# Paged decode attention: cache pages by indirect transfers, transposed on VectorE, scored in 32x32 tiles

## The chip, the cores and the metric

One core of one Trainium2 chip runs the whole program, one launch. The metric is the device time of that launch in microseconds (us), lower is better. A core has TensorE (PE, with its weight loads as PEld), VectorE (DVE), ScalarE (ACT), GpSimd (POOL) and SyncE (SP), which run their own instruction streams and meet at semaphores. All matrices are float32.

## What is computed

One inference step of a two-layer hybrid decoder: a diagonal state-space layer, then an attention layer that reads one shared compressed latent cache. It runs for a prompt of 512 tokens and for eight decode sequences of one new token each, whose 2048 past positions lie in pages. Cut to the part at issue, per decode sequence:

```
c_past   = cache_ckv[page_table]   # (8, 2048, 256), pages of 128 positions
kpe_past = cache_kpe[page_table]   # (8, 2048, 32)
s   = (q_lat @ c^T + q_pe @ kpe^T) * 96**-0.5      # 16 heads x 2049 keys
o   = softmax(s) @ c                                # 16 x 256
out = (o per head @ w_uv) @ w_o
```

Around it stand four SwiGLU feed-forward blocks, the state-space mixer, projections and norms, in three-product split precision.

## The kernel before, in words

Everything is written by hand per engine, in program order, with explicit semaphores. Prompt and decode tokens share the big products (520 columns). After the latent queries are ready, PE runs the prompt attention over eight pairs of heads (`scores`, `turned_probs`, `weighted`), and then the decode attention over eight sequences, called batches (b = 0..7) here. The output projection `w_o` follows; its first halves (`wo_half(d, 0, ...)`, 24 matmuls each, line 3209) are placed between the last steps of decode.

**Loads.** `page_loader` (before line 654) reads page numbers into registers and loads a batch's 16 pages of 128x256 into `cb[b % 3]` and 16 key pages of 128x32 into `kb[b % 3]`, split over SP (9 pages) and POOL (7), key loads at line 639. Partition p holds position p of each page. Three buffers: the load of b+3 waits until the weighted sum of b is done (`d_o`); that of batch 2 waits for the end of the prompt attention (`a_ol`).

**Decode, per batch.** PE transposes the pages with an identity (`turned`, line 2401: 36 of 128x128 in nine groups, the last for the keys) into PSUM banks 0, 1, 7; ACT (lines 1489, 1491) and DVE (line 2247) copy them in turn to `cbT` and `kbT`. Scores: line 3223 (8 matmuls of 32x512, in four column tiles, one for each quarter of the keys) and line 3227 (16 of 32x128). DVE takes the maximum (2291, 2292), ACT the exponential with the row sum (1532), PE turns the probabilities (4 transposes), DVE copies them (2301), and PE forms the weighted sum (line 3258, 16 matmuls of 32x256), which ACT copies out (1537). The PE order in round b is scores of b, first transposes of b+1, probabilities of b, other transposes of b+1, weighted sum of b:

```python
            for b in range(NB):
...
                if b + 1 < NB:
                    for q in range(4):
                        turned(b + 1, q)
...
                pe.wait_ge(d_e, b + 1)
...
                if b + 1 < NB:
                    for q in range(4, 9):
                        turned(b + 1, q)
```

A float32 matmul shows as two records in the trace.

## Time and profile before

| | us |
|---|---|
| median of 3 runs | 2009.85 |
| lowest and highest run | 2007.43, 2014.37 |
| span of the profiled execution | 2007.1 |
| PE / DVE / ACT / POOL busy | 1960.4 / 1277.0 / 820.4 / 132.8 |

The span runs from the first to the last instruction of the profiled execution; its own run time is not given apart from it, and the span is 0.33 us under the lowest run. Busy times are sums of an engine's work; a line number such as L3258 is that of the kernel above, and where a helper issues the instruction it is the helper's. Idle time of an engine that nobody waits for costs nothing.

### The profile page before, as it was taken

The numbers are of one execution on the slowest core, as the hardware profiler recorded it, in microseconds if no ns is written. First come the engines' busy times: TensorE is split into PE (matmuls) and PEld (weight loads), VectorE is DVE, ScalarE is ACT, GpSimd is POOL, SyncE is SP. The second block draws the span as 40 slices with busy tenths as digits, with TensorE's granted clock in tenths as the row PEclk, the third lists the DMA queues.
The fourth block names the chain that finished last, engine by engine and source line by source line (L and its number), as shares of the span: only waits on it lengthen the run. The fifth ranks groups of instructions, "written<-read, shape, count | busy, mean of one in ns | idle before, by whom it ended". The sixth has DMA issues, their size and how long they took to land.

```text
span 2007.1 us, 41612 instructions
## 1 busy us (share of the span) xinstructions
PE 1960.4 (98%) x17604; PEld 1875.2 (93%) x17604; DVE 1277.0 (64%) x1771; ACT 820.4 (41%) x1243; POOL 132.8 (7%) x231
## 2 busy tenths in 40 slices
PE   8999999988999999999999999999989999999999
PEld 7999999987999999999999999997666799999998
DVE  6445486697469577576884856655764349668474
ACT  5332233343245244255452534454654244345252
POOL 3002002010000000000000000000047000000000
PEclk9999999989999999999999999999999999999999
DMA  7233234864342322234322322231248422323222
GB/s 151 84 102 88 75 93 115 269 140 100 95 137 85 120 89 95 77 105 116 97 85 85 127 85 86 84 101 51 54 119 231 149 71 83 127 85 120 91 74 75
DMA packets 260624, 211.55 MB, mean 105 GB/s; under 512 B 42372, under 2 KB 235426, under 8 KB 260450
## 3 DMA queue, kind: packets, MB, share of 16 engines
q1 hardware_dynamic: 248528, 187.52, 31.9%
q0 software_dynamic: 6656, 13.69, 2.4%
q10 hardware_dynamic: 5266, 7.85, 1.2%
q8 instruction: 130, 2.13, 0.4%
q14 instruction: 44, 0.36, 0.1%
HBM read 195.29 MB, written 10.33 MB: 102 GB/s over the span
## 4 chain that ended last, share of the span: by engine, by line
PE 67%; DVE 3%; ACT 2%; issue 2%; SPq 1%; DMA 1%; DVEq 0%; ACTq 0%
PE ps L2459 25%; PE ps L2487 25%; PE ps L2388 6%; PE ps L2401 2%; PE ps L2947 1%; PE ps L3053 1%; PE ps L3209 1%; PE ps L3086 1%; SPq L654 1%; SPq L639 1%; DMA cb<-cache_ckv 1%; PE ps L2841 1%; PE ps L3030 1%; DVE wl L1668 0%; DVE xl L1619 0%
## 5 line engine op out<-in xcount | busy, mean ns | idle before, releaser
L2388 PE MATMUL ps<-xh,wh 128*128 128x260 f32 x1088 | 286.9, 285 | 2.6 <-DVE xl L1619 1.4
L2388 PE MATMUL ps<-xl,wh 128*128 128x260 f32 x1088 | 283.7, 283 | 0.0
L2487 PE MATMUL ps<-xoh,wh 128*128 128x260 f32 x992 | 281.3, 284 | 1.3 <-DVE sq L1835 1.3
L2487 PE MATMUL ps<-xoh,wl 128*128 128x260 f32 x992 | 281.0, 283 | 0.0
L2487 PE MATMUL ps<-xol,wh 128*128 128x260 f32 x992 | 280.6, 283 | 0.0
L2459 PE MATMUL ps<-xh,wh 128*128 128x260 f32 x872 | 228.8, 284 | 0.6 <-DVE wl L1668 0.6
L1067 ACT ACTIVATE wh<-rw 128x1024 fp32r<-128x1024 f32 (+1 forms) x135 | 138.8, 1029 | 218.6 <-PE ps L2459 151.7
L2459 PE MATMUL ps<-xl,wh 128*128 128x260 f32 x872 | 227.0, 282 | 0.0
L2388 PE MATMUL ps<-xh,wl 128*128 128x260 f32 x1088 | 219.3, 283 | 0.0
L990 ACT ACTIVATE wh<-raw 128x1024 fp32r<-128x1024 f32 (+1 forms) x90 | 100.4, 1116 | 283.4 <-PE ps L2388 250.5
L2388 PEld LDWEIGHTS ps<-xh,wh 128*128 128x128 f32 x1088 | 205.6, 189 | 6.9 <-issue 3.9
L2388 PEld LDWEIGHTS ps<-xl,wh 128*128 128x128 f32 x1088 | 205.1, 188 | 0.0
L1668 DVE TENSOR_TENSOR wl<-rw,wh 128x1024 fp32r<-128x1024 f32 (+1 forms) x135 | 160.3, 1188 | 67.3 <-ACT wh L1067 67.2
L2487 PE MATMUL ps<-xoh,third 128*128 128x260 f32 x1040 | 198.6, 283 | 0.6 <-DVE sq L1835 0.6
L2487 PEld LDWEIGHTS ps<-xoh,wh 128*128 128x128 f32 x992 | 186.6, 188 | 1.6 <-DVE wl L1668 1.6
L2487 PEld LDWEIGHTS ps<-xol,wh 128*128 128x128 f32 x992 | 186.9, 188 | 0.0
L2487 PEld LDWEIGHTS ps<-xoh,wl 128*128 128x128 f32 x992 | 186.8, 188 | 0.0
L1579 DVE TENSOR_TENSOR wl<-raw,wh 128x1024 fp32r<-128x1024 f32 (+1 forms) x92 | 120.5, 1310 | 89.5 <-ACT wh L990 81.8
L2459 PE MATMUL ps<-xh,wl 128*128 128x260 f32 x872 | 175.5, 283 | 0.0
L2388 PEld LDWEIGHTS ps<-xh,wl 128*128 128x128 f32 x1088 | 167.9, 189 | 0.0
L2459 PEld LDWEIGHTS ps<-xh,wh 128*128 128x128 f32 x872 | 164.4, 189 | 1.7 <-DVE wl L1668 1.1
L2487 PEld LDWEIGHTS ps<-xoh,third 128*128 128x128 f32 x1040 | 164.8, 188 | 0.8 <-DVE third L1668 0.8
(550 smaller groups left out, 4202.2 us busy)
## 6 DMA issues: line engine op xcount, KB each, us to landing
rw<-ffn_w_gate SPq DMA_DIRECT2D x33, 1024.0 KB, 5.4
rw<-ffn_w_up SPq DMA_DIRECT2D x33, 1024.0 KB, 8.0
rw<-ffn_w_down SPq DMA_DIRECT2D x12, 2048.0 KB, 7.8
raw<-ffn_w_gate SPq DMA_DIRECT2D x22, 512.0 KB, 3.9
raw<-ffn_w_up SPq DMA_DIRECT2D x22, 512.0 KB, 3.9
raw<-ffn_w_down SPq DMA_DIRECT2D x16, 704.0 KB, 4.8
rw<-ffn_w_down SPq DMA_DIRECT2D x6, 1536.0 KB, 6.7
cb<-cache_ckv SPq DMA_DIRECT2D x72, 128.0 KB, 3.7
```

The source lines that it names most:

```text
L639: eng.dma_start(kb[j][:, g, :], inp["cache_kpe"][bass.ds(numbers[b][g], 1)].rearrange("a p r -> p (a r)")).then_inc(arrived[j], 16)
L654: eng.dma_start(cb[j][:, g, :], inp["cache_ckv"][bass.ds(numbers[b][g], 1)].rearrange("a p r -> p (a r)")).then_inc(arrived[j], 16)
L990: run(wh[par_][:, 0:size], raw[par_][:, 0:size], ACT.Copy).then_inc(w_hi, 1)
L1067: run(as_slot(name, slot_h(name, n), n), raw_of(name, n), ACT.Copy).then_inc(z_hi, 1)
L1579: tt(wl[par_][:, 0:size], raw[par_][:, 0:size], wh[par_][:, 0:size], ALU.subtract).then_inc(w_lo, 1)
L1668: tt(as_slot(name, slot_l(name, n), n), raw_of(name, n), as_slot(name, slot_h(name, n), n), ALU.subtract).then_inc(z_lo, 1)
L2388: got = mm(ps[0:width, bank + half, 0:HALF], w[par_][:, k * width:k * width + width], src[:, k0 + k, half * HALF:half * HALF + HALF], star ...
L2401: return nc.tensor.transpose(dst, src, ident[0:rows, 0:rows])
L2459: got = mm(ps[:, bank + half, T0], w[:, cols], src_[:, k, half * HALF:half * HALF + HALF], start=first and m == 0 and s == 0, stop=last an ...
L2487: got = mm(ps[:, bank + mat, T0], w[:, cols], src[:, j, k, :], start=first and k == 0 and m == 0 and s == 0, stop=k == 3 and m == 1, skip_ ...
L2841: got = mm(ps[:, bank + half, 0:HALF], w[slot][:, k * P:k * P + P], src[:, k, half * HALF:half * HALF + HALF], start=k == 0 and m == 0 and ...
L2947: got = mm(ps[:, 2 * (i % 2) + half, 0:HALF], cols, src[:, k, half * HALF:half * HALF + HALF], start=k == 0 and o == 0 and s == 0, stop=k ...
```

## The change

The caches are viewed as rows of 16 positions, so that one indirect transfer per batch and cache, on POOL, brings page rows straight to the partitions: partition p holds positions 16p to 16p+15. The row numbers (page number times 8 plus p % 8) are made once, from the page table, which POOL loads in eight small transfers at the start. DVE transposes `cb` and `kb` in 32x32 blocks from SBUF to SBUF, five operations a batch (`turned(b, k)`, four of 128x1024, one of 128x512). The scores are 9 x 16 matmuls of 32 rows, 32 columns and 128 keys (`cache_scores`): row group i works on the positions that partitions 32i to 32i+31 held, 32 of the 256 + 32 dimensions at a time, and writes PSUM bank i; column group c takes four of the 16 positions of each partition. For this the queries stand four times, once per row group, in `qrep`: SP copies them from `qlat` with 16 transfers (`latent_rows`), in place of its register loads. The new token's scores have 16 columns per batch rather than 32. ACT, not DVE, copies the turned probabilities. The weighted sum of b now stands after the scores of b+1, and the projection's halves and banks are placed anew.

```diff
-SP_PG = 9
-N_SP, N_POOL = 2 * SP_PG - 1, 2 * (NPG - SP_PG) + 1
-AHEAD = 5
-LAST_EARLY = 5
+SLOT = PAST // P
+SUBS = PAGE // SLOT
 SCALE = float(DQ) ** -0.5
 HP = 32
 NQ = P // HP
 KB = PAST // NQ
+NJ = R // DR + 1
+PAIRS = tuple((2 * k, 2 * k + 1) for k in range(R // DR // 2)) + ((NJ - 1,),)
+NT = len(PAIRS)
+WO_BANK = ((7, 4), (1, 0), (2, 5), (3, 6))
 NEG = -1e30
...
-            qlat, qpe, snew = take(s, ("qlat", [P, RT, NB, HP], F32), ("qpe", [P, NB, 4, HP], F32),
-                                   ("snew", [NB, NB, HP], F32))
+            qlat, qrep, snew = take(s, ("qlat", [P, RT, NB, NH], F32), ("qrep", [P, NJ, NB * NH + NH], F32),
+                                    ("snew", [NB, NB, HP], F32))
...
-                    m, ("cbT", [P, RT, PAST], F32), ("cb2", [P, NPG, R], F32), ("mb", [P, NB], F32), ("nmb", [P, NB], F32),
+                    m, ("cbT", [P, NJ - 1, KB], F32), ("cb2", [P, NPG, R], F32), ("mb", [P, NB], F32), ("nmb", [P, NB], F32),
...
-        kbT = tb[:, 0, 0:4 * P].rearrange("p (g k) -> p g k", g=4)
+        kbT = tb[:, 0, 0:KB]
...
-        def page_loader(eng, arrived, ckv, kpe):
...
-                for g in kpe:
-                    eng.dma_start(kb[j][:, g, :], inp["cache_kpe"][bass.ds(numbers[b][g], 1)].rearrange("a p r -> p (a r)")).then_inc(arrived[j], 16)
...
-                for g in ckv:
-                    eng.dma_start(cb[j][:, g, :], inp["cache_ckv"][bass.ds(numbers[b][g], 1)].rearrange("a p r -> p (a r)")).then_inc(arrived[j], 16)
...
+            def latent_rows(i):
+
+                if i == 0:
+                    sp.wait_ge(l_qe, 1)
+                for q in range(NQ):
+                    sp.dma_start(qrep[DR * i:DR * i + DR, q:NJ - 1:NQ, 0:NB * NH],
+                                 qlat[DR * q:DR * q + DR, :, :, :].rearrange("p r b h -> p r (b h)")).then_inc(d_q, 16)
+
...
-                if i - 2 < AHEAD:
-                    number(i - 2)
+                if i - 2 < NQ:
+                    latent_rows(i - 2)
             load(WO0 + 1, (WO0 + 1) % 2, wo[:, :, P:2 * P], KD)
 
-            caches()
             sp.wait_ge(d_o, NB - 2)
...
+            def cache_out(b):
+                act.wait_ge(d_o, b + 1)
+                run(ob[:, b, :], ps[:, 5 + b % 2, 0:R], ACT.Copy).then_inc(d_oe, 1)
 
             for b in range(NB):
-                if b + 1 < NB:
-                    turned(b + 1, 0)
-                else:
-                    act.wait_ge(d_o, NB - 1)
-                    for j in range(2):
-                        act.wait_ge(w_in[(WO0 + j) % 2], slots.arrived(WO0 + 2 + j))
-                        run(w4h[:, j, :], raw[(WO0 + j) % 2][:, 0:KD * P], ACT.Copy).then_inc(w_hi, 1)
-
                 act.wait_ge(d_m, b + 1)
                 if b >= 1:
                     act.wait_ge(d_pt2, b)
-                run(pb, ps[:, 2 + b % 2, :], ACT.Exp, bias=nmb[:, b:b + 1], scale=SCALE, accum_out=lb[:, b:b + 1]).then_inc(d_e, 1)
-                if b + 1 < NB:
-                    for q in range(2, 9, 2):
-                        turned(b + 1, q)
-                act.wait_ge(d_o, b + 1)
-                run(ob[:, b, :], ps[:, 5 + b % 2, 0:R], ACT.Copy).then_inc(d_oe, 1)
+                run(pb.rearrange("p (m i k) -> p i m k", m=NQ, i=NQ),
+                    ps[:, 0:NQ, 0:P].rearrange("p i (m k) -> p i m k", m=NQ),
+                    ACT.Exp, bias=nmb[:, b:b + 1], scale=SCALE, accum_out=lb[:, b:b + 1]).then_inc(d_e, 1)
+                if b >= 1:
+                    cache_out(b - 1)
+                act.wait_ge(d_pt2, b + 1)
+                run(pbT[:, :, :], ps[:, 4, :].rearrange("p (m q) -> p m q", m=NQ), ACT.Copy).then_inc(d_pe, 1)
             act.wait_ge(d_w, 1)
             run(mrow[:, :, :], mrow[:, :, :], ACT.Exp, scale=SCALE)
             run(nrow[:, :], nrow[:, :], ACT.Exp, scale=SCALE).then_inc(d_we, 1)
+            for j in range(2):
+                act.wait_ge(w_in[(WO0 + j) % 2], slots.arrived(WO0 + 2 + j))
+                run(w4h[:, j, :], raw[(WO0 + j) % 2][:, 0:KD * P], ACT.Copy).then_inc(w_hi, 1)
+                if j == 0:
+                    cache_out(NB - 1)
...
-                    last = copy(qpe[DR * k:DR * k + DR, :, k, Q_POS[h]:NH:4], qq[DR * h:DR * h + DR, NH // 2:NQT, SEQ:TOK].rearrange("p g b -> p b g"))
+                    last = copy(qrep[DR * k:DR * k + DR, NJ - 1, 0:NB * NH].rearrange("p (b h) -> p b h", b=NB)[:, :, Q_POS[h]:NH:4], qq[DR * h:DR * h + DR, NH // 2:NQT, SEQ:TOK].rearrange("p g b -> p b g"))
...
+            def turned(b, k):
+
+                if k == 0:
+                    dve.wait_ge(d_in[b % 3], (b // 3 + 1) * 16)
+                elif k == NT - 1:
+                    dve.wait_ge(d_kin[b % 3], (b // 3 + 1) * 16)
                 if b >= 1:
-                    dve.wait_ge(d_s, b)
-                copy(cbT[:, q // 4, (q % 4) * 512:(q % 4) * 512 + 512], ps[:, (0, 1, 7)[(b * 9 + q) % 3], :]).then_inc(d_td, 1)
+                    dve.wait_ge(d_s, (b - 1) * NT + k + 1)
+                if k == NT - 1:
+                    V.transpose(kbT, kb[b % 3][:, :, :].rearrange("p s e -> p (s e)")).then_inc(d_t, 1)
+                else:
+                    j0, j1 = PAIRS[k][0], PAIRS[k][-1] + 1
+                    V.transpose(cbT[:, j0:j1, :].rearrange("p j (s k) -> p j s k", k=DR),
+                                cb[b % 3][:, :, DR * j0:DR * j1].rearrange("p s (j e) -> p j s e", e=DR)).then_inc(d_t, 1)
 
             for i in range(NH // 2):
                 more = i + 1 < NH // 2
...
-            turned(0, 3)
-            turned(0, 5)
+            turned(0, 1)
             weighted(NH // 2 - 1)
-            turned(0, 7)
+            for k in range(2, NT):
+                turned(0, k)
...
-                dve.wait_ge(d_s, b + 1)
-                own(V.tensor_reduce(mb[:, b:b + 1], ps[:, 2 + b % 2, :], AX.X, ALU.max))
+                if b + 1 < NB:
+                    turned(b + 1, 0)
+                dve.wait_ge(d_s, (b + 1) * NT)
+                own(V.tensor_reduce(mb[:, b:b + 1], ps[:, 0:NQ, 0:P], AX.XY, ALU.max))
                 ts(nmb[:, b:b + 1], mb[:, b:b + 1], -SCALE, None, ALU.mult).then_inc(d_m, 1)
                 if b + 1 < NB:
-                    turned(b + 1, 1)
-                    turned(b + 1, 3)
-                else:
-                    wide_lo(0)
-                dve.wait_ge(d_pt2, b + 1)
-                if b >= 1:
-                    dve.wait_ge(d_o, b)
-                copy(pbT[:, :, :], ps[:, 4, :].rearrange("p (m q) -> p m q", m=NQ)).then_inc(d_pe, 1)
-                if b + 1 < NB:
-                    turned(b + 1, 5)
-                    turned(b + 1, 7)
+                    for k in range(1, NT):
+                        turned(b + 1, k)
                 if b == 1:
                     dve.wait_ge(l_rdy, 1)
                     eye = ident[0:NB, 0:NB].unsqueeze(2).to_broadcast([NB, NB, HP])
...
+            def cache_scores(b, k):
+
+                if b == 0 and k == 0:
+                    pe.wait_ge(d_q, 16 * NQ * NQ)
+                    pe.wait_ge(a_e, NH // 2 * NSS)
+                pe.wait_ge(d_t, b * NT + k + 1)
+                for j in PAIRS[k]:
+                    for c in range(NQ):
+                        for i in range(NQ):
+                            rows = slice(DR * i, DR * i + DR)
+                            keys_ = kbT if j == NJ - 1 else cbT[:, j, :]
+                            got = mm(ps[HP * c:HP * c + HP, i, 0:P], qrep[rows, j, NH * b:NH * b + HP], keys_[rows, P * c:P * c + P],
+                                     start=j == 0, stop=j == NJ - 1, skip_group_check=True)
+                got.then_inc(d_s, 1)
...
-            for q in range(2, 6):
-                turned(0, q)
+            cache_scores(0, 0)
             weighted(NH // 2 - 1)
-            for q in range(6, 9):
-                turned(0, q)
+            for k in range(1, NT):
+                cache_scores(0, k)
...
+            def cache_weighted(b):
...
+            for b in range(NB):
+                if b >= 1:
+                    cache_weighted(b - 1)
+                pe.wait_ge(d_e, b + 1)
+                for m in range(NQ):
+                    got = turn(ps[:, 4, m * P:m * P + P], pb[:, m * P:m * P + P])
+                got.then_inc(d_pt2, 1)
+                if b + 1 < NB:
+                    for k in range(NT):
+                        cache_scores(b + 1, k)
+            turn(ps[0:NB, 0, 0:P], mb[:, :])
+            turn(ps[0:NB, 0, P:2 * P], lb[:, :]).then_inc(d_rt, 1)
+            pe.wait_ge(a_ol, NH // 2)
+            wo_half(0, 0, 0, 3)
+            cache_weighted(NB - 1)
+            wo_half(0, 0, 3, KD)
             pe.wait_ge(d_ws, 1)
             turn(ps[:, 4, 0:NB], mrow[:, :, :].rearrange("p q h -> p (q h)"), NB)
-            mm(ps[:, 7, NB * HP:2 * NB * HP], ones[0:NB, :], own_w[:, :, :].rearrange("p b h -> p (b h)"), start=True, stop=True).then_inc(d_wp, 1)
-            wo_half(2, 0, 3, 5)
+            mm(ps[:, 0, NB * HP:2 * NB * HP], ones[0:NB, :], own_w[:, :, :].rearrange("p b h -> p (b h)"), start=True, stop=True).then_inc(d_wp, 1)
+            wo_half(1, 0, 0, 3)
...
+            for c in range(SUBS):
+                pool.dma_start(pt[c:P:SUBS, :], inp["page_table"].rearrange("b g -> g b"), allow_slow_non_contiguous=True).then_inc(d_pt, 16)
...
+            G.memset(qrep[:, :, NB * NH:NB * NH + NH], 0.0)
+            G.memset(snew[:, :, :], 0.0).then_inc(m_zero, 1)
+            pool.wait_ge(d_pt, 16 * SUBS)
+            pool.wait_ge(c_in, 48)
+            own(G.tensor_scalar(slot_row[:, :], pt[:, :], float(SUBS), cst[:, C_SUB:C_SUB + 1], ALU.mult, ALU.add))
+
+            def rows_of(b):
+                return bass.IndirectOffsetOnAxis(ap=slot_row[:, b:b + 1], axis=0)
+
+            def keys(b):
+
+                j = b % 3
+                if b >= 3:
+                    pool.wait_ge(d_t, NT * (b - 2))
+                pool.indirect_dma_start(kb[j][:, :, :].rearrange("p s e -> p (s e)"), None,
+                                        inp["cache_kpe"].rearrange("n (u s) e -> (n u) (s e)", s=SLOT), rows_of(b)).then_inc(d_kin[j], 16)
+
+            def pages(b):
+
+                j = b % 3
+                if b == 0:
+                    pool.wait_ge(a_qs[0], 64 * (NH // 4))
+                    pool.wait_ge(a_qs[1], 64 * (NH // 4))
+                elif b == 1:
+                    pool.wait_ge(a_ve, NH // 2)
+                elif b == 2:
+                    pool.wait_ge(a_ol, NH // 2)
+                else:
+                    pool.wait_ge(d_o, b - 2)
+                pool.indirect_dma_start(cb[j][:, :, :].rearrange("p s r -> p (s r)"), None,
+                                        inp["cache_ckv"].rearrange("n (u s) r -> (n u) (s r)", s=SLOT), rows_of(b)).then_inc(d_in[j], 16)
+
+            for b in range(NB):
+                pages(b)
+                if b < 2:
+                    keys(b)
+                if b == 1:
+                    keys(2)
+                if 2 <= b < NB - 1:
+                    keys(b + 1)
```

Where instructions move, as the built programs list them (line, operation, output and inputs, shape, awaited semaphores, count). PE before, from the last transposes of batch 1 over the weighted sum of batch 0 to the scores of batch 1 (`cb`, `kb` are cache pages, `ta` the probabilities, `cst` the identity):

```order
L2401 MATMUL ps<-cst,cb 128x128 [waits dec_tr_d]
L2401 MATMUL ps<-cst,cb 128x128 x3
L2401 MATMUL ps<-cst,cb 128x128 [waits dec_tr_a]
L2401 MATMUL ps<-cst,cb 128x128 x3
L2401 MATMUL ps<-cst,kb 128x128 [waits dec_tr_d]
L2401 MATMUL ps<-cst,kb 128x128 x3
L3258 MATMUL ps<-cb,ta 32x256 [waits dec_p_sb]
L3258 MATMUL ps<-cb,ta 32x256 x15
L3223 MATMUL ps<-cbT,qlat 32x512 [waits dec_tr_d,dec_tr_a]
L3223 MATMUL ps<-cbT,qlat 32x512 x7
```

PE now, from the last scores of batch 1 over the weighted sum of batch 0 to the first scores of batch 2:

```order
L3106 MATMUL ps<-cbT,qrep 32x128 [waits dec_tr]
L3106 MATMUL ps<-cbT,qrep 32x128 x31
L3106 MATMUL ps<-tb,qrep 32x128 [waits dec_tr]
L3106 MATMUL ps<-tb,qrep 32x128 x15
L3160 MATMUL ps<-cb,ta 32x256 [waits dec_p_sb]
L3160 MATMUL ps<-cb,ta 32x256 x15
L2345 MATMUL ps<-cst,ta 128x128 [waits dec_exp]
L2345 MATMUL ps<-cst,ta 128x128 x3
L3106 MATMUL ps<-cbT,qrep 32x128 [waits dec_tr]
```

The transposes of `cb` are gone, and the weighted sum (`cb,ta`) stands behind the scores of the next batch (`cbT,qrep`) and ahead of the turned probabilities of that batch.

DVE before, one round (`mb` is the maximum, `ta` the turned probabilities):

```order
L2291 TENSOR_REDUCE mb<-ps 128x1 [waits dec_s]
L2292 TENSOR_SCALAR nmb<-mb 128x1 [waits dch]
L2247 COPY cbT<-ps 128x512 [waits dec_s,dec_tr] x2
L2301 COPY ta<-ps 128x512 [waits dec_o,dec_p_tr]
L2247 COPY cbT<-ps 128x512 [waits dec_s,dec_tr] x2
```

DVE now:

```order
L2196 STREAM_TRANSPOSE cbT<-cb 128x1024 [waits dec_s,dec_in1]
L2243 TENSOR_REDUCE mb<-ps 128x1 [waits dec_s]
L2244 TENSOR_SCALAR nmb<-mb 128x1 [waits dch]
L2196 STREAM_TRANSPOSE cbT<-cb 128x1024 [waits dec_s] x3
L2193 STREAM_TRANSPOSE tb<-kb 128x512 [waits dec_s,pool_in1]
```

A block transpose of the next batch, which waits for that batch's load (`dec_in1`), stands ahead of the maximum; four more follow it.

POOL now (it had 7 page and 8 key loads a batch here):

```order
L3409 DMA cb<-cache_ckv,slot_row 128x4096 [waits att_ol]
L3394 DMA kb<-cache_kpe,slot_row 128x512 [waits dec_tr]
L3409 DMA cb<-cache_ckv,slot_row 128x4096 [waits dec_o]
L3394 DMA kb<-cache_kpe,slot_row 128x512 [waits dec_tr]
L3409 DMA cb<-cache_ckv,slot_row 128x4096 [waits dec_o]
```

Each page load waits for a weighted sum (`dec_o`), and the key load one batch ahead follows it.

## Rows read from the trace of the kernel before

**Rows 1.** The page: span, and section 1 (busy, share, instructions).

```profile
span 2007.1 us, 41612 instructions
...
PE 1960.4 (98%) x17604; PEld 1875.2 (93%) x17604; DVE 1277.0 (64%) x1771; ACT 820.4 (41%) x1243; POOL 132.8 (7%) x231
```

**Rows 2.** Windows: busy us (instructions) of PE, PEld, DVE, ACT, POOL; clock, DMA share, GB/s.

```profile
1515.00:1525.00 10.00, 9.99 (x128) 7.05 (x131) 4.91 (x9) 4.15 (x10) 7.65 (x15) 1.00 0.61 166
1525.00:1535.00 10.00, 9.49 (x128) 6.70 (x124) 5.23 (x10) 4.00 (x9) 9.19 (x18) 1.00 1.00 274
```

**Rows 3.** Waits, 1500 to 1600: us in total, times, longest.

```profile
DVE mb L2291 <- PE ps L3227: 32.4, 8, 4.3
...
PE ps L2401 <- DMA cb<-cache_ckv: 2.1, 3, 1.0
```

**Rows 4.** Chain of waits, 1490 to 1640: start, us, what.

```profile
1534.78 1.86 PE ps L3258 x32
1536.64 1.72 PE ps L3223 x16
1538.36 0.87 PE ps L3227 x32
1539.23 1.93 PE ps L2401 x16
1541.18 2.98 PE ps L2401 x24
...
1573.95 1.86 PE ps L3258 x32
...
1577.53 0.88 PE ps L3227 x32
```

**Rows 5.** Timeline, 1495 to 1535: start, us, engine, line, what.

```profile
1506.30 0.69 DVE L2235 TENSOR_TENSOR xl<-ps,xh 128x512 fp32r<-128x512 f32 x1 [2.25 <-ACT xh L1478]
...
1515.41 1.93 PE L3258 MATMUL ps<-cb,ta 128*32 128x256 f32 x32
```

**Rows 6.** Groups by form, 1495 to 1620: count, busy us, mean ns, idle before.

```profile
L2401 PE MATMUL ps<-cst,cb 128*128 128x128 f32 x256 | 31.8, 276 | 2.1 <-DMA cb<-cache_ckv 2.1
...
L654 POOL DMA_DIRECT2D cb<-cache_ckv x42 | 22.6, 537 | 22.6 <-issue 20.1 <-PE ps L3258 0.8
...
L2291 DVE TENSOR_REDUCE mb<-ps 128x1 f32<-128x512 f32 x8 | 5.5, 691 | 32.4 <-PE ps L3227 32.4
...
L1532 ACT ACTIVATE ta<-ps,nmb 128x512 f32<-128x512 f32 x8 | 5.5, 682 | 1.2 <-DVE nmb L2292 1.2
...
L2287 DVE TENSOR_TENSOR w4l<-raw,w4h 128x1024 fp32r<-128x1024 f32 x2 | 2.4, 1220 | 0.0
...
L2292 DVE TENSOR_SCALAR nmb<-mb 128x1 f32<-128x1 f32 x8 | 1.2, 154 | 0.3
```

**Rows 7.** Small tiles: line 2853 (ns min/median/max), and a group by form.

```profile
L2853 PE MATMUL ps<-sn,ct x128: 201/201/221, 443.7 to 445.4; 128*32 128x8 f32 x128
...
L2817 PE MATMUL ps<-ctcw,xsr 64*64 64x128 f32 x256 | 7.9, 272 | 4.9 <-DVE xsr L740 4.8
```

**Rows 8.** DMA issues: count, KB each, median us to landing.

```profile
rw<-ffn_w_down SPq DMA_DIRECT2D x12, 2048.0 KB, 7.8
...
wsh<-s_w_rows POOLq DMA_DIRECT2D x1, 4096.0 KB, 23.3
```

**Rows 9.** Windows of 2 us, columns as in rows 2.

```profile
1492.00:1494.00 2.00, 0.22 (x2) 0.20 (x4) 1.90 (x9) 1.37 (x5) 1.71 (x4) 1.00 0.38 62
1496.00:1498.00 2.00, 2.00 (x12) 1.31 (x9) 0.08 (x1) 0.60 (x1) 0.00 (x0) 0.50 0.00 0
1598.00:1600.00 2.00, 2.00 (x11) 2.00 (x11) 0.46 (x3) 0.26 (x1) 0.00 (x0) 0.50 0.06 18
```

**Rows 10.** Chain of waits, the output projection.

```profile
1585.10 3.09 PE ps L3209 x24
...
1597.75 5.80 PE ps L3209 x36
```

More of the change, by code:

```diff
@@ L87 @@
 C_E4 = C_S32 + HP
-C_COLS = C_E4 + NQ
+C_SUB = C_E4 + NQ
+C_COLS = C_SUB + 1
 C_GRP, C_ALL = C_COLS, C_COLS + D
@@ L287, in yoco_step @@
         wl = take(ctx, *[(f"wl{j}", [P, HF * P], F32R) for j in range(2)])
[L290 removed]
+        be0, lst, pt, slot_row = take(ctx, ("be0", [P, KD, P], F32), ("lst", [P, 3, 4, NPAIR], F32), ("pt", [P, NB], I32), ("slot_row", [P, NB], I32))
         with ExitStack() as s:
@@ L1452, in _ @@
             act.wait_ge(l_s, 1)
-            run(snew[:, :, :], ps[0:NB, 6, 0:NB * HP].rearrange("p (b h) -> p b h", b=NB), ACT.Copy).then_inc(l_rdy, 1)
+            act.wait_ge(m_zero, 1)
+            run(snew[:, :, 0:NH], ps[0:NB, 6, 0:NB * NH].rearrange("p (b h) -> p b h", b=NB), ACT.Copy).then_inc(l_rdy, 1)
             def softmax(i, n):
@@ L1481, in _ @@
                 softmax(0, n)
-            def turned(b, q):
-                act.wait_ge(d_t, b * 9 + q + 1)
-                if b >= 1:
-                    act.wait_ge(d_s, b)
-                src = ps[:, (0, 1, 7)[(b * 9 + q) % 3], :]
-                if q < 8:
-                    run(cbT[:, q // 4, (q % 4) * 512:(q % 4) * 512 + 512], src, ACT.Copy).then_inc(d_ta, 1)
-                else:
-                    run(kbT[:, :, :], src.rearrange("p (g k) -> p g k", g=4), ACT.Copy).then_inc(d_ta, 1)
             for i in range(NH // 2):
@@ L2252, in _ @@
                     maximum(i + 1, 0)
+                else:
+                    turned(0, 0)
                 if i == 0:
@@ L2268, in _ @@
                     normalise(i + 1, 2)
-                else:
-                    turned(0, 1)
                 probs(i, 5)
@@ L2328, in _ @@
                ps[:, 4, 0:NB].unsqueeze(2).to_broadcast([P, NB, HP]), ALU.mult).then_inc(d_fin, 1)
-            own(copy(nwt[:, :, :], ps[:, 7, NB * HP:2 * NB * HP].rearrange("p (b h) -> p b h", b=NB)))
+            own(copy(nwt[:, :, :], ps[:, 0, NB * HP:2 * NB * HP].rearrange("p (b h) -> p b h", b=NB)))
             wide_lo(1)
@@ L3185, in _ @@
                 turned_probs(i, 3)
-                if not more:
-                    turned(0, 0)
                 turned_probs(i, 4)
-                if not more:
-                    turned(0, 1)
                 turned_probs(i, 5)
```

143 lines of the change are left out of this document (19 added, 124 removed).

## The prediction

> **What bounds the kernel now.** The page comes first [rows 1]: TensorE (PE) is busy for 98% of the span of 2007.1 us, so work that is taken from it counts, unless a wait takes its place. The change touches one stage, the decode attention of eight sequences ("batches" here), so the windows of that stage come next [rows 2]: the granted clock is 1.00 (2.4 GHz), PE is busy 9.5 to 10 of 10 us, and the DMA share is 0.61 to 1.00 at 166 to 274 GB/s. Two limits therefore lie close together, and relief of one meets the other. The waits say the same [rows 3]: VectorE (DVE) stands 32.4 us waiting for PE's scores, while PE waits 2.1 us for cache pages, three times.
>
> The chain of waits gives one batch in steps [rows 4]: weighted sum 1.86 us, scores against the latent 1.72, scores against the rotary key 0.87, 1.93 for 16 transposes and 2.98 for 24 more (20 of the cache, 4 of the probabilities). The weighted sum of batch 0 begins at 1515.41 [rows 5] and that of batch 6 at 1573.95 [rows 4]: 58.54 us over 6 is **9.76 us a batch**. The scores of batch 7 end at 1577.53 + 0.88 = **1578.4**, the mark of my sum. After it the output projection keeps PE supplied, as it will afterwards.
>
> **The change, part by part.**
>
> *Transposes leave PE.* 36 of 128x128 a batch at 31.8 us / 256 for the latent [rows 6], 0.124, hence 4.5 us of PE. Their nine evacuations on ACT and DVE go too.
>
> *Scores in small tiles.* 24 matmuls (2.6 us in rows 4) become 9 x 16 = 144 of 32x32 tiles and 128 columns; each shows as two records, 288 a batch. The rotary scores, four column tiles of 128 columns at once, took 0.87 us for 32 records [rows 4], 0.109 for four. If sixteen run at once, 18 groups take **2.0 us**; if only four do, 72 groups take 7.8. The nearest rows [rows 7]: 64x64 tiles, two row groups and two column groups at once, 256 records in 7.9 us busy, which without row concurrency would need twice that; and 128 small records within 1.7 us, 13 ns each. 288 x 13.3 ns is 3.8 us. I take 2.0 to 3.8: either is hidden beside the next part, and 7.8 is a rival.
>
> The same row speaks to a rule against this change. The Trainium skill (TensorE: Matmul & The Clock Gate, section "Wait — 56ns, not 53.3ns?") says that where instructions are not decoded in hardware the sequencer spends about 62 ns on each matmul. By that rule 144 matmuls would be an estimated 8.9 us a batch and the kernel would be slower. The 13 ns a record of rows 7, 27 a matmul, speak against it here.
>
> *Transposes on DVE.* Four of 128x1024 and one of 128x512 a batch. No such operation is in the trace. The nearest are a DVE operation from SBUF on 128x1024, 1220 ns, and the maximum, 691 ns for 512 out of PSUM [rows 6]. I take 1.15 us and 0.6; the bounds are 0.6 us (twice that rate) and 2.2 us (half of it). With the maximum (0.69 + 0.15) DVE has 4 x 1.15 + 0.6 + 0.85 = 6.0 us a batch, under 9.76.
>
> *Order.* DVE now has the first transpose of batch b+1 ahead of the maximum of batch b, so that softmax b waits for the landing L of b+1. From L: 1.15 + 0.85 + 3 x 1.15 + 0.6, and 0.3 for the last matmuls: scores b+1 end at L + 6.35. Only then comes the weighted sum of b, w = 1.86 at full clock, which releases the buffer that load b+3 waits for. The old order had that sum ahead of the next scores. With T from issue to landing, **L(b+3) = L(b+1) + 6.35 + w + T**: two batches per round.
>
> *The loads.* 16 page loads and 16 key loads a batch from two queues become two indirect ones from POOL. SP and POOL issues (0.54 us each on POOL [rows 6]) vanish; but nothing starts before the buffer is free, and the whole 2 MB must land before the first transpose. The nearest rows [rows 8]: 2048 KB from SP lands in 7.8 us; a 4096 KB load from POOL's queue in 23.3, that is 11.7 for half. I take **T = 8.4**, nearest to the first, which has the same size, with 7.0 (the 2.36 MB at somewhat over the 274 GB/s of rows 2, and no more) and 11.7 as ends. The data alone, 2.36 MB at the 274 GB/s of rows 2, would be 8.6 a batch, as much as the loop above (6.35 + 2.35 + 8.4 over two batches, 8.55), so a second limit stands close behind; larger pieces should pass it. The skill (DMA: Bandwidth & Descriptors, section "Anatomy of one DMA — SWDGE (gpsimd) path") gives 2.0 us plus bytes over 436 GB/s, an estimated 6.8 us for this load; by it the sum would be about 5 us lower. No row here reaches that rate.
>
> *PE's clock.* From the weighted sum's end, L(b) + 8.7, to the turned probabilities, L(b+1) + 2.8, PE will idle 2 to 3 us a batch. In the trace a gap of this kind left its mark [rows 9]: PE busy 0.22 of 2 us at 1492, and a granted clock of 0.50 (1.2 GHz) at 1496, with PE fully busy. At that level a weighted sum takes 3.7; I take w = 2.35, a quarter of them low. The projection will also start low once: where the clock fell to 0.50 at 1598 [rows 9], 36 records took 5.80 us against 3.09 for 24 at 1585 [rows 10], that is 1.2 us more than their share.
>
> *Head.* The DVE evacuation of the last prompt head begins at 1506.30 [rows 5]; without cache transposes ahead of the last weighted sum it should be 1.3 us sooner, ending at 1505.7. Three transposes follow (1.15, 1.15, 0.6), so that scores 0 end at 1508.8. The first transpose of 1 (to 1509.7), the maximum (to 1510.6) and the rest give scores 1 at 1515.0, weighted sum 0 at 1516.8 and the issue of load 3 there. L(3) = 1516.8 + T. Load 2 (from 1505.7 to 1514.1) is in time. The new token's scores shrink from 256 to 128 columns: 3 x 0.2, 0.6 us saved. The page-table issues on POOL, the replication of queries by SP (16 small DMAs) and the removed register loads lie in those queues' idle time: nothing.
>
> *Sum.* L(7) = L(3) + 2 x (6.35 + w + T); after it scores 7 (6.35) and weighted sum 6 (w), which stood before the mark in the old order: 1516.8 + 19.05 + 3 x (w + T) = 1535.9 + 3 x 10.75 = 1568.1, against 1578.4: -10.3. With -0.6 and +1.2: **-9.7 us**, a span of 1997.4. The span of 2007.1 is 2.75 below the median of 2009.85 (the lowest run is 2007.43), so the median becomes **2000.2**. The last few tens of microseconds hold no other change: softmax 7 hides behind weighted sum 6, and the chain from row sums to weights (about 4.3 us) behind half a projection tile (3.09 for 24 records, [rows 10]) and a weighted sum, 4.9.
>
> **Rivals.**
>
> 1. *Loads slow.* The indirect load needs 11.7 us or more, as the POOL row suggests. Each microsecond of T costs three: 3 x 3.3 = 9.9, hence +0.2 us, 2010.1, no change; at 14 us it would be +7.1, 2017. For: it is the same queue. Against: the SP row, and that the 4096 KB load is cut into short rows. Chance 0.16.
>
> 2. *Slower: DVE becomes the bound.* A transposed block of 4-byte elements passes at half the rate, 2.2 us per 1024. Then DVE has 4 x 2.2 + 1.1 + 0.85 = 10.8 us a batch. Scores 0 end at 1512.5, scores 7 at 1512.5 + 7 x 10.8 = 1588.1, with w 1589.9: +11.5, with -0.6 and +1.2 **+12.1, 2022.0**. It decides from about 1.6 us per transpose on. For: no row shows the operation. Against: every DVE row here runs near one element per cycle and lane. Chance 0.13.
>
> 3. *Small tiles bind PE.* They run four at a time, or their issue is the limit: 7.8 us of scores, with 0.44 and 1.86 10.1 a batch on PE. Scores 0 would end near 1511: 1511 + 7 x 10.1 + 1.9 = 1583.6, 5.2 past the mark, less 0.6: +4.6, 2014.5. Rows 7 speak against it. Chance 0.07. The 62 ns of the page above would be this rival, somewhat dearer.
>
> 4. *Everything fast.* T at 7.0 and w at 1.86, as PE stays at 2.4 GHz: 1535.9 + 26.6 = 1562.5, -15.9, with -0.6 and no low start -16.5, 1993.3. For: the 1 KB pieces of before cost more per byte than long ones should. Chance 0.12. The 6.8 us of the page above lead here.
>
> **How the numbers follow.** My forecast has 0.52. About 6 us (0.3%) is what a measurement of this kernel can tell from no change; the forecast's own spread of T (up to 10) gives 2005.0 at its upper end, so some of it counts as no change. Faster: 0.45 of the forecast and all of rival 4, 0.57. No change: 0.07 of the forecast, 0.10 of rival 1, 0.02 of rival 3, 0.19. Slower: the rest of these, 0.11, and rival 2, 0.24. The range runs from 1993 (rival 4) to 2018 (rival 1 at 14 us) and leaves out most of rival 2.
>
> **What would show it.** Right: STREAM_TRANSPOSE groups of 1.1 to 1.2 us; score records at 7 to 14 ns; cache loads landing in 8 to 9 us; 8.5 us from one weighted sum to the next; PE idle 2 to 3 us a batch, ended by DVE's transposes after a DMA; a granted clock under 1 in the stage. Wrong: landings of 11 us and more, transposes of over 1.6 us, or DVE never waiting for a load; also a clock that stays low far into the projection, which I count at 1.2 us only.

## The result, and the profile after

The changed kernel takes a median of 2033.4 us (2030.06 to 2037.92, 4 runs) against 2009.34 us (2007.43 to 2014.37, 4 runs) before it: ratio 1.0114, 95% interval 1.0096 to 1.0131. It is slower by 24 us, where 2000.2 was forecast, and lies above the range. The profiled run took 2030.06 us, its span is 2028.2.

The page, sections 1 and 2, against [rows 1]:

```profile
span 2028.2 us, 43625 instructions
...
PE 1954.6 (96%) x19236; PEld 1868.7 (92%) x19236; DVE 1290.5 (64%) x1771; ACT 802.4 (40%) x1211; POOL 87.7 (4%) x136
```

TensorE has 1632 matmul records more and is busy 6 us less, in a span that is 21 us longer: it stands still. The windows say where, columns as in [rows 2]:

```profile
1515.00:1525.00 10.00, 9.08 (x309) 5.40 (x294) 6.29 (x9) 1.76 (x4) 1.91 (x2) 0.63 0.12 25
1525.00:1535.00 10.00, 4.75 (x200) 2.93 (x180) 2.59 (x4) 0.58 (x1) 0.00 (x0) 0.71 0.53 218
```

PE was busy 9.99 and 9.49 us here, now 9.08 and 4.75, and its clock is low for over half of the time. What it waits for, 1500 to 1600 (us in total, times, longest), against [rows 3]:

```profile
ACT ta L1468 <- DVE nmb L2244: 73.8, 8, 10.7
POOL cb L3409 <- PE ps L3160: 55.7, 5, 14.4
DVE cbT L2196 <- DMA cb<-cache_ckv,slot_row: 34.4, 6, 7.7
...
PE ps L3106 <- issue: 23.3, 8, 5.2
```

L3106 is the score matmul of 32x32, L3160 the weighted sum, L2196 the transpose on DVE. The last row is the finding: for 23.3 us PE waited at a score matmul for nothing that another engine owed it ("issue"); a ninth wait of that kind, 2.4 us, lies inside a weighted sum, so **25.7 us** in all. The waits of DVE, ACT and POOL follow from it only in part: in fewer_scores below, which has no such gap, they are still 19.8, 54.6 and 39.0 us, from the order and the loads. The chain of waits over one batch, against [rows 4]:

```profile
1522.47 0.59 PE ps L2345 x4
1523.06 3.83 PE ps L3106 x208
1526.88 5.25 issue
1532.13 0.74 PE ps L3106 x31
1532.87 3.48 PE ps L3160 x32
```

For scores and weighted sum a batch needs 3.83 + 0.74 + 3.48, and 5.25 us of nothing between two score matmuls of the rotary keys, the first of which had already run. The weighted sum of batch 0 begins at 1518.90, that of batch 6 at 1595.23 and ends at 1598.24:

```profile
1518.90 3.57 PE ps L3160 x32
...
1595.23 3.01 PE ps L3160 x32
1598.24 0.80 PE ps L2345 x6
```

That is (1595.23 - 1518.90) / 6 = **12.7 us a batch** instead of 9.76, and the mark is 1598.24 instead of 1578.4, 19.8 later. From the mark to the end of the span it is 430.0 us against 428.7 before. Of the 21.1 us by which the span grew, 19.8 lie ahead of the mark.

The DMA view of 1500 to 1600 offers a cause: a queue of its own carries instructions, in packets of 16384 bytes. After, then before (packets, MB, share):

```profile
q8 instruction: 20, 0.33, 1.3%
```

```profile
q8 instruction: 10, 0.16, 0.7%
```

TensorE's program holds 648 instructions a batch now (576 of scores: each matmul has two weight loads and two passes; 64 of the weighted sum, 8 of turns) and 240 before. 240 in 9.76 us with a packet every 10 us makes about 250 instructions a packet (an estimate), so that a batch now needs 2.6 packets. In the trace two packets never begin less than 3.3 us apart. Where a cache load begins, the next packet starts 5.9 to 8.4 us after the one before, and the one after it 3.5 to 4.8 us later. Eight of the nine gaps end 1.3 to 1.5 us after a packet is in, the ninth 1.0. For the gap of 5.25 us, 1526.88 to 1532.13: from 1521.5 to 1529.5 the DMA view lists the load and no packet of q8, and from 1529.5 to 1532.2 it lists the one after which PE goes on:

```profile
q0 software_dynamic: 119, 1.95, 64.5%
```

```profile
q0 software_dynamic: 103, 0.41, 37.7%
q8 instruction: 1, 0.02, 2.2%
```

### The profile page after: what moved, and what is told of

It reads as the page before. It is cut to its first block, busy times and chain, and to the rows that moved or that the text cites. A ratio compares the mean times of both kernels' runs of the same rounds, so it can differ in the third digit from the quotient of the medians.

```text
span 2028.2 us, 43625 instructions
## 1 busy us (share of the span) xinstructions
PE 1954.6 (96%) x19236; PEld 1868.7 (92%) x19236; DVE 1290.5 (64%) x1771; ACT 802.4 (40%) x1211; POOL 87.7 (4%) x136
## 4 chain that ended last, share of the span: by engine, by line
PE 66%; DVE 4%; issue 3%; ACT 2%; DMA 1%; POOL 0%; DVEq 0%; POOLq 0%; ACTq 0%
PE ps L2431 24%; PE ps L2403 24%; PE ps L2332 6%; PE ps L2345 1%; PE ps L2891 1%; PE ps L2997 1%; PE ps L3106 1%; PE ps L3146 1%; PE ps L3030 1%; DMA cb<-cache_ckv,slot_row 1%; PE ps L3160 1%; PE ps L2785 1%; DVE xl L1561 1%; PE ps L2974 1%; DVE wl L1610 0%
```

## The experiments

**Theory F**: TensorE runs out of fetched instructions. Rivals: **C**, the array's time in small tiles, doubled by the low clock; **I**, slow execution of many small instructions, fetched or not (the rival 3 of the prediction); **O**, the order of the work together with the load's duration. The kernel before ran beside each group of experiments and had medians of 2009.3 to 2012.0 us, so that the ratios compare better than the times.

**short_columns**: the same instructions, a quarter of the latent columns.

```
-  mm(ps[.., i, 0:P], .., keys_[rows, P * c:P * c + P], ..)
+  w = P if j == NJ - 1 else P // 4
+  mm(ps[.., i, 0:w], .., keys_[rows, P * c:P * c + w], ..)
```

> The changed kernel, with the latent scores' 128 matmuls a batch kept in number, tiles and order, but each over 32 columns instead of 128 (three quarters of the latent scores are left out; the rotary scores overwrite the rest). Theory F (TensorE runs out of fetched instructions: in the changed kernel 648 instructions a batch against 240, blocks of 16384 bytes on the instruction queue at least 3.5 us apart, gaps ended by 'issue' of 25.7 us in the stage): the number of instructions is the same, so the gaps stay at 20 to 30 us and the time at 2026 to 2036. Rival C (the array's own time in small tiles, at half the clock half of the time, is what costs): a quarter of the columns takes 1.5 to 3 us a batch off, the time falls to 2010 to 2020. Rival O (the order of weighted sum and scores, with loads of 9.3 us, sets 12.7 us a batch by itself): 2033, with gaps that are only slack.

Measured 2034.03 us (3 runs), ratio to before 1.0104 (1.0082 to 1.0127), the same as the change. Waits of 1500 to 1600:

```profile
PE ps L3107 <- issue: 30.2, 10, 5.2
...
PE ps L3161 <- issue: 3.0, 1, 3.0
```

Three quarters of the latent scores' array work bought nothing: C falls. The gaps grew to 33.2 us, since less work lies between the same number of instructions.

**fewer_scores**: 48 score matmuls of unchanged shape.

```
-  for c in range(NQ):
+  for c in range(NQ if j == NJ - 1 else 1):
```

> The changed kernel, with the latent scores given only to the first of four column tiles: 48 score matmuls a batch instead of 144, of unchanged shape (three quarters of the latent scores are left out). Transposes on VectorE, loads and order are unchanged. Theory F: 264 instructions a batch, about what the kernel before had; no gap over 0.5 us ended by 'issue' in the scores, weighted sums 8.5 to 9.3 us apart, the sum of my prediction with T = 9.3 comes true, 2000 to 2008. Rival C: the time falls too, since array work goes as well, but no lower than by 1.5 to 3 us a batch, 2010 to 2020. Rival O: stays at 2028 to 2036, since order and loads are the same.

2007.92 us (8 runs), 0.9984 (0.9970 to 0.9997). No wait of a PE matmul on issue is left. 25 us are gained by leaving out matmuls whose array time, by short_columns, costs nothing: against O, and for F or I, which this run can't tell apart. But 9.76 us a batch is slower than the 9.0 that my loop gives with T = 9.3, and 2000 was not reached (below).

**long_columns**: one matmul over 512 columns for four over 128.

```
-  for c in range(NQ): for i in range(NQ):
-      mm(ps[HP * c:HP * c + HP, i, 0:P], .., keys_[rows, P * c:P * c + P], ..)
+  for i in range(NQ):
+      mm(ps[HP * i:HP * i + HP, 0, :], .., keys_[rows, :], ..)
```

> The changed kernel, with the score matmuls of each 32-row tile run once over 512 columns, in the column tile of the same number, instead of four times over 128 columns: 36 matmuls a batch instead of 144, four tiles at work instead of sixteen, the same column count streamed per row tile in all (the keys of a head then stand in other rows than the weighted sum takes them, so the attention over the cache is another one). Theory F: 208 instructions a batch; the gaps go, scores last about 0.85 us for each pair of j at full clock for half of the matmuls' number, time 1998 to 2008. Rival C: only 4 of 16 tiles work, the array needs four times as long per score, so the time is higher than 2033: 2035 to 2050. Rival O: 2028 to 2036.

2023.34 us (6 runs), 1.0071 (1.0044 to 1.0098). The gaps are gone, and yet a batch takes 11.5 us: the scores now keep PE busy for 59.9 + 8.3 us in eight batches, 8.5 each. So the first half of F's expectation held and its time did not, and C's 2035 to 2050 did not come either. The 7.8 us that the prediction gives for four tiles at a time is near what this kernel pays, but it is not the cause in the changed one. (The program has 216 instructions a batch, not the 208 that the expectation counted.)

**before_cut_columns** and **before_cut_finer**: the kernel before, with its latent score matmuls cut into 4 and into 16.

```
-  for c in range(NQ):
-      mm(ps[.., 2 + j, :], .., cbT[:, r, KB * c:KB * c + KB], start=r == 0, ..)
+  for u in range(0, KB, 32):
+      for c in range(NQ):
+          mm(ps[.., 2 + j, u:u + 32], .., cbT[:, r, KB * c + u:KB * c + u + 32], start=r == 0 and u == 0, ..)
```

(cut_columns: pieces of 128, each with its own start of accumulation, by which part of the products of the first latent half is left out.)

> The kernel before, with each latent score matmul of 512 columns cut into four of 128: 432 instructions a batch instead of 240, the same columns streamed. Theory F: gaps ended by 'issue' appear inside the scores and the transposes of the stage, where the kernel before has none of 0.5 us, 1 to 3 us a batch, and the time rises by 10 to 30 us. Rivals C and O: at 13 ns a record the latent scores take at most 3.3 us instead of 1.72, 0 to 13 us in all, and there is no such gap.

> The kernel before, with each latent score matmul of 512 columns cut into sixteen of 32: 720 instructions a batch instead of 240. before_cut_columns had 336 (not 432, as its expectation counted; four columns cuts of 8 matmuls add 96) and no gap. Theory F: at 3.3 to 3.8 KB of instructions per us a batch of 46 KB needs 12 to 14 us instead of 9.76: issue gaps of 10 to 30 us in the stage, time 2024 to 2044. Rival I (execution alone, 13.3 ns for each of 256 matmul records instead of 1.72 us): at most 1.7 us a batch more, no gap, 2009 to 2023.

before_cut_columns: 2008.63 us (one run) and no gap. My count was wrong, as the second expectation says, and 336 instructions a batch don't starve the engine: 10 to 30 us were expected, nothing came. before_cut_finer: 2056.39 us (2 runs), **1.0227** (1.0194 to 1.0259), more than I expected; no DVE transpose, no indirect load and no small tile is in it, and it has the gaps:

```profile
PE ps L3224 <- issue: 14.0, 7, 3.0
PE ps L3228 <- issue: 5.5, 2, 3.1
```

These are 19.5 us up to 1600, and three more gaps up to 1623 add 7.0. The time rose by 44 to 47 us, so that 18 to 20 us are not gaps. The clock was lower, too (0.88 from 1500 to 1600, against 0.99 before); no run divides the rest. Executing the small pieces isn't what costs: the latent scores keep PE busy for 21.9 us in eight batches, 2.7 each, where rival I allowed 3.4.

**short_loops**: as many matmuls executed, fewer in the program.

```
-  for j in PAIRS[k]: (16 matmuls of j)
+  with pe.Fori(0, 2): (16 matmuls of j = PAIRS[k][0])
```

> The changed kernel, with the two equal halves of each latent piece (32 score matmuls for two j) written as a loop of two turns over the first j's 16 matmuls; the second j of each pair is left out of the scores and the first counted twice (in piece 0 once). TensorE executes as many matmuls as in the changed kernel, of the same shape, in the same order, but its program holds 392 instructions a batch instead of 648. In the trace of the kernel before, TensorE's loops of the feed-forward layers (250 to 350 us) run 1700 records without one fetched block. Theory F (fetching is what starves TensorE): gaps ended by issue under 5 us in all instead of 25.7, 6 fetched blocks in 1500 to 1550 instead of 10, time 2004 to 2014. Rival I (TensorE's sequencer is slow at so many small matmuls, fetched or not): gaps as before, 2028 to 2038.

2016.5 us (2009.08 to 2021.75, 10 runs), 1.0023 (1.0006 to 1.0040): 17 us under the changed kernel with the same 648 instructions executed in a batch. No PE matmul waits for issue in 1500 to 1600, and the queue carries less:

```profile
q8 instruction: 14, 0.23, 0.9%
```

This separates F from I: with the same matmuls executed, fetching fewer of them gives back 17 of the 24 us and every gap. Executing them isn't free, though: short_loops stays 8.6 us above fewer_scores, which executes a third as many score matmuls. Its time is also above the 2014 that I had put as the end, and 7 packets came up to 1550, where I expected 6. The low clock doesn't tell these kernels apart: from 1500 to 1600 it is 0.83 here, 0.83 in the changed kernel and 0.82 in fewer_scores.

**quarter_loads** and **loads_in_quarters**: do the packets queue behind the cache loads?

```
-  pool.indirect_dma_start(cb[j][:, :, :], .., rows of 16 slots)
+  if b < 3: (as before)  else: pool.indirect_dma_start(cb[j][:, 0:4, :], .., rows of 4 slots)
```
```
+  for q in range(4):
+      pool.indirect_dma_start(cb[j][:, 4 * q:4 * q + 4, :], .., rows of 4 slots)
```

> The changed kernel, with the cache load of batches 3 to 7 cut to the first 4 of the 16 slots of each row (512 KB instead of 2 MB; the other slots keep what an earlier batch left, so three quarters of these caches are left out). All instructions of TensorE and VectorE stay. Theory F1 (TensorE runs out of instructions because the fetched blocks of 16384 bytes queue behind the cache load: 3.5 us from one block to the next without a load, 6.4 to 8.4 beside one): blocks come 3.4 to 4 us apart throughout, the issue gaps fall from 25.7 us to under 10, a batch takes 9 to 10 us, the time is 2000 to 2012. Rival F2 (the supply of instructions is what it is, loads or not): gaps of 20 us or more and 2025 to 2034. What this run can't tell is how much of the gain is the shorter wait for the load itself; the gaps ended by issue tell it.

> The changed kernel, with each cache load issued as four indirect loads of 4096 bytes a row instead of one of 16384 (same bytes, same rows). If the fetched blocks wait for single long packets of the load, F1 says that with shorter packets they come sooner: gaps of 5 to 15 us instead of 25.7, time 2012 to 2026; three more issues on the gather queue, 0.95 us each, delay the landing by up to 2.9 us. If they wait for the whole load that stands ahead of them, whatever its packets, or for the bandwidth, nothing changes but the landing: 2030 to 2042.

quarter_loads: 2018.7 us (3 runs), 1.0044 (1.0021 to 1.0067), 10.8 us a batch, packets 3.3 to 4.8 us apart for most of the stage:

```profile
PE ps L3106 <- issue: 16.8, 9, 4.3
...
PE ps L3160 <- issue: 0.2, 1, 0.2
```

Under 10 us of gaps and at most 2012 us were expected, 17.0 and 2018.7 came: the loads beside it cost a part (25.7 to 17.0), the supply alone is too slow as well. loads_in_quarters: 2031.75 us (4 runs), 1.0091 (1.0073 to 1.0109): in time, shorter packets of the load change nothing that could be told from the changed kernel. The gaps fell to 18.7 us, but waits for the exponential rose from 3.6 to 10.5 us, and a batch took 13.7 us in the profiled run (2037.72, the slowest of the four). Whether it is the load's queue or the memory behind it that delays the instructions stays open.

**sum_first** and **fewer_sum_first**: the order.

```
 DVE  -  turned(b + 1, 0); maximum(b); turned(b + 1, 1..4)
      +  maximum(b); turned(b + 1, 0..4)
 PE   -  weighted(b - 1); turns(b); scores(b + 1, 0..4)
      +  turns(b); weighted(b); scores(b + 1, 0..4)
```

> The changed kernel, with the maximum of batch b ahead of all transposes of b+1 on VectorE, and the weighted sum of b on TensorE directly behind its turned probabilities, ahead of the scores of b+1; same instructions in number. Theory F: 648 instructions a batch still have to be fetched at about 3.3 KB per us, 12 to 13 us a batch, 2026 to 2038. Rival O (the order of the changed kernel, in which softmax b waits for load b+1 and the buffer comes free late, costs most of it): 2000 to 2015.

> The order of sum_first together with the 48 score matmuls a batch of fewer_scores (three quarters of the latent scores left out). In fewer_scores TensorE was idle 7.0 to 7.3 us once in two batches, behind two cache loads that ran at the same time, and the time was 2007.9. If that is the order's doing (my loop of two batches a round), the loads now follow one another and VectorE sets the pace with 4 x 1.22 + 0.64 + 0.84 us: 6.6 to 8 us a batch, time 1986 to 1996. If it is the loads' own rate, the wait stays and the time is 2003 to 2010.

sum_first: 2055.62 us (2 runs), 1.0217 (1.0197 to 1.0238), worse by 22 us, where F had 2026 to 2038 and O a gain: both missed. In the chain each batch now has the softmax in the open, the wait for the exponential and that for its evacuation, in series with the issue gap:

```profile
1540.51 1.53 PE ps L3104 x59
...
1542.13 0.70 DVE mb L2241
1542.86 0.17 DVE nmb L2242
1543.04 0.79 ACT ta L1468 x2
...
1543.88 1.13 PE ps L2343 x4
1545.02 0.61 ACT ta L1472
...
1545.67 3.64 PE ps L3158 x32
1549.31 3.05 PE ps L3104 x134
...
1554.63 4.87 issue
```

While PE stands, the supply doesn't catch up for the next scores (17.7 us of gaps at the scores instead of 23.3). fewer_sum_first: 2004.86 us (5 runs), 0.9967 (0.9954 to 0.9980), 8.3 us a batch. That is not the 1986 to 1996 expected of the order, though no wait of DVE for a cache load is left from 1500 to 1600: PE waits 14.5 us for the exponential and 4.8 us for its evacuation, so softmax in series with scores and sum sets the pace, not VectorE. The gain over fewer_scores is only 3 us in the median, since this order also leaves the last softmax uncovered: weighted sum 7 begins 9.6 us after weighted sum 6, in fewer_scores 3.8.

**block_queries** and **block_order**: what the finding suggests is fewer, wider matmuls. Scores with the queries block by block on the diagonal need two matmuls for each j instead of sixteen. The order changes with it: as in sum_first the maximum stands ahead of the transposes, and the weighted sum of b comes behind scores (b+1, 1) rather than behind all of them.

```
-  sixteen mm(ps[HP * c.., i, 0:P], qrep[rows, j, ..], keys_[rows, P * c:P * c + P])
+  for c in range(2):
+      mm(ps[64 * c:64 * c + 64, b % 2, 0:256], q_diagonal[:, j, 0:64], keys_[:, 256 * c:256 * c + 256])
+  mm(ps[:, 2, 0:8], per_head, mx8)                      # one maximum for all groups of a head
+  32 mm(ps[DR * i.., 3, 32 columns], pb[:, 32 columns], ident[:, 32 columns])   # turns
```

> A version meant to beat both: the changed kernel's cache loads and VectorE transposes, but the sixteen 32x32 tiles for each j become two matmuls of 128 rows, 64 columns of queries and 256 keys, with the queries of a batch standing block by block on the diagonal (zero elsewhere), so that each 32-row block still meets only its own keys; the 16 heads fill the columns, the maximum and the exponential see 256 columns instead of 512. Since one head now lies in eight partition groups, a matmul with a 0/1 matrix gives all of them one maximum. The probabilities are turned by 32 matmuls of 32x32 into the order of the cache rows. 268 instructions a batch instead of 648. Theory F: no issue gap over 0.5 us in the stage; TensorE's work is 3.9 (scores, from 2048 columns in 1.72 us of the kernel before at four tiles, here 4608 at two) + 1.9 (weighted sum) + 1 to 1.7 (turns), 7 to 7.6 us a batch; VectorE's 4 x 1.22 + 0.64 + 0.35 + 0.4 = 6.3; weighted sums 7.5 to 8.8 us apart instead of 12.7 (9.76 before), time 1990 to 2003, faster than both. If the order and the loads bind (the 9.7 us a batch of fewer_scores), 2003 to 2010; if theory F is wrong and each small matmul stalls by itself, over 2010.

> block_queries with another order, since TensorE there stood still twice a batch (0.8 us for the maximum, 0.85 us for the first transpose) and a batch took 10.2 us, of it 5.1 of scores, 1.95 of weighted sum and 1.0 of turns. On VectorE the first transpose of b+1 again stands ahead of maximum b, the second ahead of the common maximum; on TensorE scores (b+1, 0) stand ahead of the 0/1 matmul of b, (b+1, 1) ahead of the turns, (b+1, 2) ahead of the weighted sum. If these two gaps are what binds, 8.5 to 9.0 us a batch and 2000 to 2007 (7 x 1.3 us less than block_queries, 2015.8). If the loads bind, because the weighted sum now frees the buffer later, 9.5 us a batch or more and 2008 to 2016.

block_queries: 2015.78 us (10 runs), 1.0028 (1.0016 to 1.0040), against 1990 to 2003 expected. No gap of fetching inside the batches, but 10.2 us a batch: the scores took 20.1 + 18.6 + 4.8 us in eight batches, 5.4 each instead of 3.9, and PE stood twice a batch. block_order takes these two waits out of the way: **2006.04 us** (1999.23 to 2010.35, 10 runs), **0.9977** (0.9964 to 0.9989), 8.9 us a batch, both inside what was expected. It leaves nothing out and beats both kernels, the one before (2010.79 beside it) by 4.7 us; that is under 0.3%, but the interval excludes 1. What still binds it, 1500 to 1600:

```profile
PE ps L3138 <- DVE cbT L2222: 9.8, 12, 2.3
DVE cbT L2222 <- DMA cb<-cache_ckv,slot_row: 9.7, 6, 3.5
```

All kernels in one table. Instructions are those of TensorE's program; a batch is the mean from the start of weighted sum 0 to that of 6; gaps are PE matmuls waiting for issue at scores and weighted sum, 1500 to 1600.

| kernel | instructions a batch | us a batch | per us | gaps, us | time, us |
|---|---|---|---|---|---|
| before | 240 | 9.76 | 25 | 0 | 2009.3 |
| before_cut_columns | 336 | 9.7 | 35 | 0 | 2008.6 |
| before_cut_finer | 720 | 14.8 | 49 | 19.5 | 2056.4 |
| changed | 648 | 12.7 | 51 | 25.7 | 2033.4 |
| short_columns | 648 | 12.7 | 51 | 33.2 | 2034.0 |
| loads_in_quarters | 648 | 13.7 | 47 | 18.7 | 2031.8 |
| sum_first | 648 | 16.1 | 40 | 18.1 | 2055.6 |
| quarter_loads | 648 | 10.8 | 60 | 17.0 | 2018.7 |
| short_loops | 392 (648 executed) | 10.5 | 37 | 0 | 2016.5 |
| fewer_scores | 264 | 9.8 | 27 | 0 | 2007.9 |
| fewer_sum_first | 264 | 8.3 | 32 | 0.5 | 2004.9 |
| long_columns | 216 | 11.5 | 19 | 0 | 2023.3 |
| block_queries | 268 | 10.2 | 26 | 1.3 | 2015.8 |
| block_order | 268 | 8.9 | 30 | 1.3 | 2006.0 |

Up to 37 instructions per us nothing starves for more than 0.5 us, sum_first does at 40; with full cache loads no kernel got beyond 51, with quarter loads 60. (The 1.3 us of the last two is one gap, ahead of the first scores.)

## Why the prediction was wrong, point by point

- **Scores in small tiles: the step that failed.** I counted 288 records of 13.3 ns, 3.8 us, hidden beside DVE, and put the supply of instructions at nothing. The size is right where PE is fed at the full clock: 64 records in 1.07 us, and the scores end on time in batch 0, at 1508.5 as forecast (1508.8):

```profile
1502.88 1.07 PE L3106 MATMUL ps<-cbT,qrep 32*32 32x128 f32 x64
```

  Over the whole stage it was too low as well: the scores keep PE busy for 5.1 us a batch in the changed kernel and 5.4 in short_loops. What I left out is that every instruction must first be fetched. I took the price of a record from a short burst [rows 7], 128 records of 8 columns that, as I read it now, were there already, and multiplied. In a stage that needs 2.6 packets a batch, one after another, the bursts run dry, for 25.7 us in all.

  The miss is 33.2 us (2033.4 against 2000.2). By the medians, 16.9 of them are the fetching (down to short_loops, 2016.5), 8.6 the execution of the other two thirds of the score matmuls (down to fewer_scores, 2007.9), and 7.7 the loop and its loads (down to the forecast). These are rough steps, since each kernel leaves something out and waits overlap; the two steps behind the fetching hold the low clock, too.
- **Rival 3** bore the right name, PE bound by issue, with the wrong mechanism (a time for each instruction) and so about a quarter of the loss: 5.2 us past the mark, 19.8 measured, chance 0.07. Execution has a share, 8.6 us by the steps above, but not by running four at a time. The rule that stands beside it, about 62 ns for each matmul where they are not decoded in hardware (the Trainium skill, TensorE: Matmul & The Clock Gate, section "Wait — 56ns, not 53.3ns?"), is not what happens here: 64 records of 32 matmuls in 1.07 us are 33 ns a matmul at most, and short_loops executes as many matmuls without a gap.
- **Transposes on DVE**: 1.15 and 0.6 us taken, 1.22 and 0.67 measured. Right within 6 to 12%, rival 2 (2.2 us) fell:

```profile
L2196 DVE STREAM_TRANSPOSE cbT<-cb 128x1024 f32<-128x1024 f32 x31 | 36.7, 1220 | 34.4 <-DMA cb<-cache_ckv,slot_row 34.4
...
L2193 DVE STREAM_TRANSPOSE tb<-kb 128x512 f32<-128x512 f32 x6 | 4.0, 669 | 0.0
```

- **Loads**: T = 8.4 taken, 9.3 measured, inside the bounds; three times 0.9, 2.7 us on the path. The estimate of 6.8 us by the Trainium skill (DMA: Bandwidth & Descriptors, section "Anatomy of one DMA — SWDGE (gpsimd) path") was further off.

```profile
cb<-cache_ckv,slot_row POOLq DMA_INDIRECT x6, 9.3
```

- **The order as a loop of two batches** can be judged in fewer_scores, where nothing starves. Load 4 was issued 5.2 us after load 3, ran beside it and landed 10.3 us after its issue (DVE starts on it at 1537.46), load 7 landed in 9.7; from landing to the end of the weighted sum it took 9.1 to 10.1 us, not 8.7. A round is 19.5 us, not 17.1, three of them 7 us:

```profile
1521.93 0.95 POOL L3409 DMA_INDIRECT cb<-cache_ckv,slot_row  x1 [9.54 <-PE ps L3160]
1527.18 0.95 POOL L3409 DMA_INDIRECT cb<-cache_ckv,slot_row  x1 [3.04 <-PE ps L3160]
...
1560.22 0.95 POOL L3409 DMA_INDIRECT cb<-cache_ckv,slot_row  x1 [11.82 <-PE ps L3160]
```

  So even without the gaps, and with two thirds of the score matmuls left out, the change is worth about nothing (2007.9): the loop's 9.76 us a batch are by chance PE's 9.76 of before. The forecast of 10.3 us at the mark was too high by most of itself, apart from the main miss.
- **PE's clock**: the weighted sum took 2.8 to 3.6 us in five of eight batches, near the 3.7 of the low level, where I had it low in a quarter. In the kernel whose order I had costed it as 2.35, fewer_scores, it is 1.93 in seven of eight. The clock is not higher there (0.82 from 1500 to 1600, 0.83 in the changed kernel, 0.99 before): its low stretches fall on the scores instead. No run shows that the gaps made the low stretches longer.
- **Head and tail** came out near: -0.6 and +1.2 around the mark, 1.3 measured behind it; nothing of page table, replication of queries or register loads shows.
- **"What would show it"** named landings, transposes and the clock. Gaps ended by nothing but issue were not on the list, though the diff put 408 instructions more into every batch of an unrolled program, and the order listing showed each of them.

## What to carry to other kernels

Count instructions, not only their time: where an edit multiplies TensorE's instructions in unrolled code, divide them by the stage's time and look at the packets of the instruction queue before and after; here 37 per us was harmless, 40 was not always, and some 50 was the ceiling beside large loads. A duration read from a burst of a few dozen instructions is not a rate. Fewer and wider matmuls, or a loop, take the gaps away, and only then do order and loads decide.
